# Output projection of an mLSTM block: pairs of weight units as one 512-column operand, and the rows' transpositions in batches behind whole tiles

## The reference

```python
mod = silu(c) @ ada_w + ada_b
sh1, sc1, g1, sh2, sc2, g2 = split(mod, 6)
h = rms_norm(x) * (1.0 + sc1) + sh1
y = mlstm_mixer(h, ml_w_in, ml_b_if, ml_norm_w, ml_w_out)   # ends in  out @ w_out
x = x + g1 * y
h = rms_norm(x) * (1.0 + sc2) + sh2
x = x + g2 * swiglu(h, w_gate_up, w_down)
return rms_norm(x) * final_norm_w
```

## Time and profile before

| | us |
|---|---|
| median of 3 runs (lowest, highest) | 1117.61 (1117.46, 1118.28) |
| the profiled execution, and its span | 1117.69, 1115.9 |
| TensorE busy | 1093.0 (98%) |
| TensorE loading weights | 927.9 (83%) |
| VectorE busy | 693.0 (62%) |
| ScalarE busy | 429.6 (38%) |
| GpSimd busy | 184.3 (17%) |
| granted TensorE clock over the span | 0.999 |

### The profile page before, as it was taken

One profiled execution on the slowest core, in us unless ns is written; L12 is line 12 of the kernel. 1 busy time (PEld: TensorE's weight loads), 2 busy tenths in 40 slices (PEclk: granted clock), 3 DMA queues, 4 the chain that ended last, 5 costly groups with the idle time before them and its releaser, 6 DMA issues.

```text
span 1115.9 us, 15219 instructions
## 1 busy us (share of the span) xinstructions
PE 1093.0 (98%) x5517; PEld 927.9 (83%) x5517; DVE 693.0 (62%) x1171; ACT 429.6 (38%) x767; POOL 184.3 (17%) x152
## 2 busy tenths in 40 slices
PE   4999999999999999999999999999999999999997
PEld 4799888888888899988888888888888888888886
DVE  5957745455456735776676767566766564944676
ACT  6772321321222522453333333333333334544344
POOL 5633312212325532730000000000000000000000
PEclk9999999999999999999999999999999999999999
DMA  9415633432531532112646354536443779755653
GB/s 367 166 59 176 187 93 95 146 95 76 156 114 57 192 111 95 77 38 79 214 156 202 101 192 149 186 100 217 142 157 136 265 262 390 250 189 190 198 159 151
DMA packets 87194, 178.17 MB, mean 160 GB/s; under 512 B 8120, under 2 KB 31288, under 8 KB 86096
## 3 DMA queue, kind: packets, MB, share of 16 engines
q1 hardware_dynamic: 86416, 175.07, 46.3%
q0 software_dynamic: 704, 2.13, 0.6%
HBM read 137.02 MB, written 40.16 MB: 159 GB/s over the span
## 4 chain that ended last, share of the span: by engine, by line
PE 56%; DVE 1%; ACT 0%; issue 0%; DVEq 0%
PE OP L2081 26%; PE O L2081 15%; PE ST L2081 5%; PE DC L2081 5%; PE AD L2081 5%; PE ST L1863 0%; PE O L1863 0%; DVE hL L1245 0%; DVE x L1708 0%; DVE tL L1245 0%; DVE x L1715 0%; ACT junk L1029 0%; DVE x L1698 0%; ACT hH L1023 0%; DVE sB L1667 0%
## 5 line engine op out<-in xcount | busy, mean ns | idle before, releaser
L1834 PE MATMUL OP<-wH,hH 128*128 128x256 f32 (+1 forms) x448 | 151.1, 337 | 0.8 <-DVE hL L1348 0.8
L1834 PE MATMUL OP<-wH,hL 128*128 128x256 f32 (+1 forms) x448 | 147.5, 329 | 0.0
L1834 PE MATMUL OP<-wL,hH 128*128 128x256 f32 (+1 forms) x448 | 147.4, 329 | 0.0
L1617 DVE TENSOR_TENSOR dL<-dF,dH 128x1024 fp32r<-128x1024 f32 x77 | 93.0, 1223 | 69.9 <-ACT dH L1077 69.0
L1077 ACT CAST dH<-dF 128x1024 fp32r<-128x1024 f32 x77 | 79.8, 1052 | 89.0 <-DMA dF<-w_units 40.3
L2081 PE MATMUL OP<-tH,wsH 128*128 128x512 f32 x264 | 103.1, 390 | 0.0
L2081 PE MATMUL OP<-tL,wsH 128*128 128x512 f32 x264 | 102.9, 390 | 0.0
L2081 PE MATMUL OP<-tH,wsL 128*128 128x512 f32 x264 | 102.9, 390 | 0.0
L1834 PEld LDWEIGHTS OP<-wH,hH 128*128 128x128 f32 x448 | 85.1, 190 | 7.8 <-DVE hL L1348 1.0
L1834 PEld LDWEIGHTS OP<-wH,hL 128*128 128x128 f32 x448 | 85.0, 190 | 7.8
L1834 PEld LDWEIGHTS OP<-wL,hH 128*128 128x128 f32 x448 | 85.2, 190 | 6.8
(11 more groups left out here) (311 smaller groups left out, 2695.6 us busy)
## 6 DMA issues: line engine op xcount, KB each, us to landing
raw<-w_units SPq DMA_DIRECT2D x76, 512.0 KB, 4.6
dF<-act_mid SPq DMA_DIRECT2D x77, 256.0 KB, 2.7
ada<-ada_rest SPq DMA_DIRECT2D x64, 256.0 KB, 2.9
wst<-w_units SPq DMA_DIRECT2D x44, 256.0 KB, 4.8
down_mid<-wst SPq DMA_DIRECT2D x22, 512.0 KB, 3.2
dF<-down_mid SPq DMA_DIRECT2D x44, 256.0 KB, 2.9
dF<-w_units SPq DMA_DIRECT2D x33, 256.0 KB, 5.9
ada<-ada_first SPq DMA_DIRECT2D x8, 1024.0 KB, 10.3
```

What stands on the lines that cost most here:

```text
L1617: nc.vector.tensor_tensor(dL[g][:], dF[g][:], dH[g][:].bitcast(F32), ALU.subtract).then_inc(d_L, 1)
L1834: ins = nc.tensor.matmul(out_ap, lhs[a], rhs[b], start=(n == 0 and i == 0), stop=(last and i == 2))
```

## The change

Two weight units are now one moving operand where both are there: for token tile t, columns of j and j+1 are computed as one tile of 24 matmuls with 512 columns, which fills a PSUM bank and is added to the residual by one instruction. The list of tiles is (j, w, t), w units wide:

- first: (0, 1, 0), pairs (0, 2, t) for t = 1 to 5, then single tiles of j = 0 for t = 6, 7 and of j = 1 for t = 0, 6, 7: 11 tiles;
- second: pairs (2, 2, t) for seven positions of `TOKENS`, and single tiles of j = 2 and j = 3 for the last: 9 tiles.

20 tiles in place of 32. The pair 0 and 1 lies in slots 0 and 1, the pair 2 and 3 in slots 0 and 2 (`slice(0, 3, 2)`); for that the units 14 and 15 swap their columns (`OUT_COLUMNS`). Tile 1 now also needs unit 13. `TR_FIRST` has seven places in place of eight, each behind a whole tile of the second list, with the same 14 entries; T1 and T2 of token tile 4 go in one batch with Q22 of token tile 5. VectorE scales row p behind the add of the whole pair p+1; ScalarE and SP wait for `Y_DONE[t]`. The splits of units 14 and 15 stand behind tile 4's and tile 8's add. The diff, without two changes of counts (SP's `save_rows` waits for `Y_DONE[t]`, the first gate-up products for `y_ev` counted from `N_Y`):

```diff
@@ -59,7 +59,9 @@
-    return [(j, t) for j in range(2) for t in range(NT)] + [(j, t) for t in TOKENS for j in (2, 3)]
+    first = [(0, 1, 0)] + [(0, 2, t) for t in range(1, 6)] + [(0, 1, 6), (0, 1, 7)] + [(1, 1, t) for t in (0, 6, 7)]
+    second = [(2, 2, t) for t in TOKENS[:-1]] + [(2, 1, TOKENS[-1]), (3, 1, TOKENS[-1])]
+    return first, second
@@ -70,8 +72,8 @@
-    first = {4: operand_tiles(0), 6: operand_tiles(1), 8: operand_tiles(2), 10: operand_tiles(3),
-             11: [("T1", 4), ("T2", 4)], 12: operand_tiles(4), 14: operand_tiles(5), 15: [("T1", 5), ("T2", 5)]}
+    first = {2: operand_tiles(0), 3: operand_tiles(1), 4: operand_tiles(2), 5: operand_tiles(3),
+             6: [("T1", 4), ("T2", 4)] + operand_tiles(4), 7: operand_tiles(5), 8: [("T1", 5), ("T2", 5)]}
@@ -86,8 +88,11 @@
-Y_SEQ = y_sequence()
-Y_AT = {jt: n for n, jt in enumerate(Y_SEQ)}
+Y_FIRST, Y_SECOND = y_sequence()
+Y_SEQ = Y_FIRST + Y_SECOND
+N_Y, N_Y1 = len(Y_SEQ), len(Y_FIRST)
+Y_DONE = {t: n + 1 for n, (_, _, t) in enumerate(Y_SEQ)}
+OUT_COLUMNS = (0, 1, 3, 2)
@@ -370,7 +375,8 @@
                         sp.wait_ge(w_L, u * 2 - 1 + i)
-                    sp.dma_start(piece(raw, i), w_units[u, i]).then_inc(raw_in[i], 16)
+                    src = U_OUT + OUT_COLUMNS[u - U_OUT] if u >= U_OUT else u
+                    sp.dma_start(piece(raw, i), w_units[src, i]).then_inc(raw_in[i], 16)
@@ -662,7 +668,7 @@
                     rv = piece(raw, i).rearrange("p (k n) -> p k n", n=DV)
-                    j = u - U_OUT
+                    j = OUT_COLUMNS[u - U_OUT]
@@ -1018,7 +1024,7 @@
                     if kind == "T3" and t == 4:
-                        act.wait_ge(y_mm, 4 * NT)
+                        act.wait_ge(y_mm, N_Y)
@@ -1103,11 +1109,12 @@
             for p, t in enumerate(TOKENS):
-                high(TR_FIRST.get(2 * p, ()))
-                act.wait_ge(y_ev, Y_AT[3, t] + 1)
+                high(TR_FIRST.get(p, ()))
+                act.wait_ge(y_ev, Y_DONE[t])
...
                 row_root(NT + p, NT + t)
-                high(TR_FIRST.get(2 * p + 1, ()))
+                if p == NT - 1:
+                    high(TR_FIRST[NT])
@@ -1483,12 +1490,12 @@
-                j, t = Y_SEQ[n]
+                j, w, t = Y_SEQ[n]
...
                 dve.wait_ge(y_mm, n + 1)
-                cols = slice(j * DV, (j + 1) * DV)
-                nc.vector.tensor_tensor(x2[:, t, cols], x2[:, t, cols], Y_BANKS[n % 4][:, 0:DV],
+                cols = slice(j * DV, (j + w) * DV)
+                nc.vector.tensor_tensor(x2[:, t, cols], x2[:, t, cols], Y_BANKS[n % 4][:, 0:w * DV],
@@ -1504,9 +1511,9 @@
             y_tile(NT - 1)
-            for n in range(NT, 2 * NT):
+            for n in range(NT, N_Y1):
                 y_tile(n)
-                if n == NT + 1:
+                if n == NT:
@@ -1715,18 +1722,19 @@
             for p, t in enumerate(TOKENS):
-                y_tile(2 * NT + 2 * p)
+                y_tile(N_Y1 + p)
...
                     norm_row(p - 1)
-                low(TR_FIRST.get(2 * p, ()))
-                y_tile(2 * NT + 2 * p + 1)
+                low(TR_FIRST.get(p, ()))
+                if p == NT - 1:
+                    y_tile(N_Y - 1)
...
                 row_inverse(NT + p, NT + t)
-                low(TR_FIRST.get(2 * p + 1, ()))
+            low(TR_FIRST[NT])
@@ -2049,17 +2057,24 @@
             def y_tile(n):
-                j, t = Y_SEQ[n]
-                if n in (0, NT, 2 * NT, 2 * NT + 1):
-                    pe.wait_ge(w_L, 2 * (U_OUT + j) + 2)
-                if j == 0:
+                j, w, t = Y_SEQ[n]
+                unit = {0: 0, 1: 1, N_Y1: 3}.get(n)
+                if unit is not None:
+                    pe.wait_ge(w_L, 2 * (U_OUT + unit) + 2)
+                if n < NT:
...
                     pe.wait_ge((th_ok, th_ok, c_ok, ad_ev)[n], (NH * NT, NH * NT, NH * (NT - 1), 2 * NH)[n])
-                ws = unit_weights(j % 3, DV)
-                project(Y_BANKS[n % 4][:, 0:DV], h_tile(t), lambda k: tuple(w[:, k, :] for w in ws)).then_inc(y_mm, 1)
+                if w == 2:
+                    slots = slice(0, 2) if j == 0 else slice(0, 3, 2)
+                    project(Y_BANKS[n % 4][:], h_tile(t),
+                            lambda k: tuple(u[:, slots, k * DV:(k + 1) * DV] for u in (wH, wL))).then_inc(y_mm, 1)
+                else:
+                    i = (0, 1, 0, 2)[j]
+                    project(Y_BANKS[n % 4][:, 0:DV], h_tile(t),
+                            lambda k: tuple(u[:, i, k * DV:(k + 1) * DV] for u in (wH, wL))).then_inc(y_mm, 1)
@@ -2069,10 +2084,10 @@
                     out_transposes(t + 2)
-            for n in range(NT, 2 * NT):
+            for n in range(NT, N_Y1):
                 y_tile(n)
-            for m in range(2 * NT):
-                y_tile(2 * NT + m)
+            for m in range(N_Y - N_Y1):
+                y_tile(N_Y1 + m)
...
```

More of the change, by code:

```diff
@@ L476, in save_rows @@
                 t = TOKENS[p]
-                sp.wait_ge(y_ev, Y_AT[3, t] + 1)
+                sp.wait_ge(y_ev, Y_DONE[t])
                 sp.dma_start(x_mid[t], x2[:, t, :]).then_inc(x_in[t], 16)
@@ L2094, in up_product @@
                     else:
-                        pe.wait_ge(y_ev, 4 * NT - 3 + n)
+                        pe.wait_ge(y_ev, N_Y - 3 + n)
                 elif q == 2:
@@ L2100, in up_product @@
                     else:
-                        pe.wait_ge(y_ev, 4 * NT - 1 + n)
+                        pe.wait_ge(y_ev, N_Y - 1 + n)
                 elif q == 5:
```

## The result

The changed kernel takes 1120.05 us (median of 12 executions, 1118.09 to 1121.67), the kernel before beside it 1117.49 (12, 1116.95 to 1118.78). The ratio of the two is 1.0021, with a 95% interval of 1.0012 to 1.003: 2.3 us slower (the medians are 2.6 apart). The forecast was 1118.5, 0.95 us slower, in a range of 1115.9 to 1120.4. The profiled execution took 1119.96 us.

The account below looks back on a forecast made before the run. TensorE, busy nearly throughout, was taken as the bound. First half zero, second half 1.45 us later less 0.5 coming back: +0.95 on 1117.69 gives 1118.6, on the median's scale 1118.5; range 1115.9 to 1120.4.

Parts of the forecast that it names:

- The pair's pace: Output projection: 512-column matmuls start 0.2267 us apart, so a pair takes 5.44 us instead of 5.76, 0.32 less.
- Tile 1 waits for unit 13.: First half: tile 1, now a pair, waits for VectorE's split of unit 13 and starts at 374.53, 2.27 later.
- First half: zero.: First 11 tiles: five pairs save 1.6 us against tile 1's late start; the end stays at 420.60.
- Weights in time.: First half: unit 15's split, moved back, runs 415.4 to 417.7 and is wanted at 420.59; cover 2.9 us.
- GpSimd's chain sets two waits.: Second half: TensorE waits for GpSimd's shifts near 455 (2.35 us) and 468 (2.07), about 4.4 us together.
- 0.5 us come back behind the second product.: Transpositions among the gate-up products: 0.5 of the 1.45 us delay returns, since an earlier wait for a low part goes.
- rival D: Projection pairs: two halves in one operand give nothing, a pair takes 5.76 us; 1121.4 us, chance 0.04.
- A: Second half: the row work keeps up and the 3.1 us saving arrives whole; 1114.5 us, chance 0.13.
- B's lighter collisions: Second half: VectorE and GpSimd collide less, TensorE waits 0.25 and 1.65 us; 1116.5 us, chance 0.11.
- C: Second half: the port stays with whoever has the next instruction ready, making shifts late; 1120.2 us, chance 0.14.

Follow-up runs that it names:

- The filled wait: Changed kernel with 24 throwaway matmuls of 256 columns in TensorE's wait before tile 1: 1118.87 us, ratio 1.0012 to the kernel before.
- the narrow tile: Changed kernel with tile 1 as a single 256-column tile and its column block 1 computed later: 1117.56 us, ratio 0.9998 to the kernel before.
- the execution in which the clock did not fall: Profile of the changed kernel with VectorE's scaling of each row directly behind its reciprocal: 1121.57 us, ratio 1.0036 to the kernel before.
- The halved shift: Changed kernel with GpSimd's shift on 512 of a row's 1024 columns, for measuring only: 1117.23 us, ratio 0.9994 to the kernel before.
- the second half alone: First half as in the kernel before, second half as in the changed kernel: 1118.09 us, ratio 1.0003 to the kernel before.
- the best kernel: Changed kernel with narrow tile 1, earlier scaling, row 5's shift before row 4's sums, last row's scaling behind the bank evictions: 1114.22 us, ratio 0.9969.
- the execution of 2838 us named above: One of two executions left out of the best kernel's first run, whose result was 1114.07 us, ratio 0.9966 to the kernel before.

## Why the prediction was right, and where not

The time lies in the range and moved the way the forecast's 0.95 us point. But it moved 2.3 us, and the forecast had given "slower by over 0.2%" a chance of 0.18 only. That it lies in the range is in part luck: a missing term of 1.7 us and a chain summed 0.65 too long had opposite signs, and without the second the median would have been some 1120.7, above the range. By the steps:

- **The pair's pace** (0.2267 a matmul, also for slots 0 and 2). Right: pairs of the second half take 5.44 to 5.47 us, and 5.55 to 5.57 behind transpositions, waits left out. The sign named for rival D, over 5.5 us, had left out the 0.08 that the sum gave to the first matmul behind transpositions; D's own price was 5.76 a pair. D is out.
- **Tile 1 waits for unit 13.** Right in place and size: 374.41 against 374.53, a wait of 3.02 us.
- **"First half: zero."** This is the step that failed. Its sum left out what a wait of 3 us can do to the pace behind it: the granted clock fell to half, which cost 1.7 us. The first half ended at 422.27, not 420.60. The filled wait and the narrow tile show it, and so does the execution in which the clock did not fall: with the same wait its first half ended at 420.75. The rows of the kernel before had only waits of 0.8 us in this stage, at full clock, and I bounded the cost of a wait by its own length.
- **Weights in time.** Right: unit 15's split ended at 419.4, wanted at 422.27; cover 2.9 us as said. TensorE never waits for it.
- **GpSimd's chain sets two waits.** Right in mechanism and place, 3.3 us instead of 4.4. The chain was mis-sized by 0.65: against the sum plus the first half's 1.67 (470.38 + 1.67 = 472.05) the last shift ended at 471.40. The scaling of row 3 came (452.19) just before the third sum (452.49) and not in the middle of the second, so it cost GpSimd 0.84 and not 1.1, and the splits 0.45 and 0.41 instead of 0.6 each. The halved shift shows that the chain is GpSimd's, the second half alone that its waits don't depend on the first half.
- **0.5 us come back behind the second product.** Right: +2.53 becomes +2.01.

In all, 0.95 + 1.7 (clock) - 0.65 (chain) = 2.0, where the third product has +2.01. The last 0.3 come behind it: a wait of 0.4 us at 581 for an add of VectorE, less 0.1 elsewhere. What causes it was not tried. This is the sum of the profiled execution; by the other profiles with this wait, the clock's term would be anything from 0 to 2.8 us in another.

Of the rivals, A was the saving that GpSimd withheld; the best kernel, with one pair less and other orders, starts the products 3.35 us earlier where A had 3.07. B's lighter collisions are a part of the truth (0.65 of its 2.1). C, the port kept by whoever is next, didn't happen: the shift of row 0 took 2.71 us from 435.48, one split's turn, not three.

## What to carry to other kernels

When an edit makes the bottleneck engine wait 3 us, look at the clock behind the wait as well as at the wait. Here it cost between nothing and 2.8 us on top, depending on the execution, so one trace doesn't give its price. A tile that needs nothing late, or throwaway matmuls in the gap, took it away. When units of work get coarser, every instruction that stood "behind the first half of the next unit" moves back by half a unit; count the side engine's work between its fixed places before counting the main engine's saving. And an order that is right for all rows but the last needs the last row looked at alone.

## What the runs showed of the hardware

- TensorE's granted clock: in the changed kernel 3.02 us idle, then 0.50 for some 3 us, though a matmul stream had started again (1.3 us before the fall; in the kernel with only the first half changed the half clock was there from the second matmul on, at 374.95). Behind 366 us the profiles of this case have seven waits of 2.87 to 4.21 us, and the half clock followed six of them; it followed none of the waits up to 1.75 us. The length of a wait doesn't decide by itself: 3.03 us before tile 1 left the clock at 1.00 once, and so did 4.23 us at 16 us from the start in the kernel before, where 4.54 us at the same place in another kernel had 0.50 behind it. The executions of the changed kernel spread by 3.6 us, those of the kernel before by 1.8; that this fall is the reason was not tried.
- VectorE's scaling, which reads two SBUF operands, and GpSimd's sums run one at a time: 1.29 became 2.13 us, 1.28 became 2.07. The Trainium skill (SBUF — State Buffer, "SBUF: two separate sides") calls what the two share an exclusive lock, held for the whole instruction; the traces agree. In the meetings read here the waiting engine had the next turn, also against an instruction queued right behind the one that ended.
- In the execution of 2838 us named above, 24 matmuls of 512 columns took 14.36 us, 0.598 each, at a granted clock of 1.00, while VectorE's busy time, 692.6 us, was the usual one (693.0 before). No run says why.
